# Two weight slabs of a layer's input projection computed inside the DeltaNet scans as native float32 products

## What is computed

```python
def even_mixer(...):
    def prepare(h):
        p = h @ w_in                                   # the input projection, (768 x 1024) @ (1024 x 6656 + 64)
        u = centred_depthwise_conv_silu(p[..., :EV_CONV], conv_w, conv_b)
        z = p[..., EV_CONV:EV_CONV + EV_GATE]          # 2048 gate columns
        small = p[..., EV_CONV + EV_GATE:]             # 64 decay and step inputs
        q, k, v, xs, bm, cm = jnp.split(u, EV_CONV_SPLITS, axis=-1)
        ...
    # DeltaNet scans, both directions, 8 heads;  SSD scans, both directions, 16 heads
    def merge(o_dn, y_ssd, x_ssd, z):
        z_dn, z_ssd = jnp.split(z, [DN_VW], axis=-1)
        o_dn = rms_norm(o_dn, dn_norm) * jax.nn.silu(z_dn)
        y = (y_ssd + ssd_d * x_ssd) * jax.nn.silu(z_ssd)
        ...
# DeltaNet, per chunk:  t = (I + A)^-1 by substitution;  u = t @ (v beta);  w = t @ (k beta exp(g))
```

## Time and profile before

| | us |
|---|---|
| median of 3 runs (lowest, highest) | 2743.19 (2742.74, 2743.46) |
| profiled execution: first to last instruction (span) | 2736.6 |
| median less span: start and end of the execution, which the trace doesn't cover | 6.6 |
| TensorE busy, share of the span | 2536.9, 93% |
| VectorE busy, share of the span | 1610.3, 59% |
| GpSimd busy, share of the span | 955.6, 35% |
| stage in0, about | 60 to 508 |
| DeltaNet g = 0, g = 1, about | 508 to 660, 660 to 803 |

### The profile page before, as it was taken

The page is one execution under the profiler, slowest core; times in us unless marked ns, Lnnn a source line. Parts: engine busy times, 40 slices in busy tenths (PEclk is TensorE's granted clock), DMA queues, the critical chain, the costliest instruction groups (busy, mean ns, idle before and its releaser), DMA issues.

```text
span 2736.6 us, 41739 instructions
## 1 busy us (share of the span) xinstructions
PE 2536.9 (93%) x15718; PEld 2257.2 (82%) x15718; DVE 1610.3 (59%) x2541; ACT 1141.0 (42%) x2081; POOL 955.6 (35%) x515
## 2 busy tenths in 40 slices
PE   7999999868588899899999999999889999899999
PEld 5999999767575588899999987989678877888887
DVE  4988886465867841877777768632666663411111
ACT  4444432435457531433233335433666664322221
POOL 2322223444536522265455533232200012344443
PEclk9999999979799999999999999999999999999999
DMA  7344455203011031123333432333674312132222
GB/s 280 112 139 132 136 168 212 82 25 127 25 45 49 28 135 62 53 94 129 126 132 131 140 107 95 133 104 112 229 244 130 128 34 71 64 106 93 92 99 86
DMA packets 126079, 307.19 MB, mean 112 GB/s; under 512 B 12640, under 2 KB 40800, under 8 KB 124512
## 3 DMA queue, kind: packets, MB, share of 16 engines
q1 hardware_dynamic: 103888, 258.36, 27.9%
q10 hardware_dynamic: 22032, 46.67, 4.9%
HBM read 249.10 MB, written 55.84 MB: 111 GB/s over the span
## 4 chain that ended last, share of the span: by engine, by line
PE 64%; DVE 15%; issue 12%; ACT 6%; POOL 2%; ACTq 1%; DMA 1%; DVEq 0%; SPq 0%; POOLq 0%
PE ps L563 12%; PE ps L564 12%; PE ps L565 12%; DVE ybuf L2785 4%; PE ps L1500 3%; PE ps L1502 3%; PE ps L1501 3%; PE ps L1401 2%; PE ps L1377 2%; PE ps L1387 2%; ACT prb L2160 1%; POOL Wl L544 1%; DVE ps L2858 1%; DVE Vall L2862 1%; DVE ps L2697 1%
## 5 line engine op out<-in xcount | busy, mean ns | idle before, releaser
L544 POOL TENSOR_TENSOR Wl<-raws,Wh 128x2048 fp32r<-128x2048 f32 (+3 forms) x129 | 504.4, 3911 | 1374.3 <-ACT Wh L538 1366.1
L563 PE MATMUL ps<-Hh,Wh 128*128 128x384 f32 (+2 forms) x1152 | 401.8, 349 | 20.9 <-ACT ubuf L1695 12.5
L565 PE MATMUL ps<-Hh,Wl 128*128 128x384 f32 (+2 forms) x1152 | 392.6, 341 | 0.0
L564 PE MATMUL ps<-Hl,Wh 128*128 128x384 f32 (+2 forms) x1152 | 392.6, 341 | 0.0
L538 ACT ACTIVATE Wh<-raws 128x2048 fp32r<-128x2048 f32 (+3 forms) x131 | 209.5, 1600 | 190.7 <-PE ps L565 140.7
L3116 DVE SCALAR_TENSOR_TENSOR xT<-ps,mod,xT 128x384 f32<-128x384 f32 (+3 forms) x174 | 84.5, 534 | 276.2 <-PE ps L565 276.2
L563 PEld LDWEIGHTS ps<-Hh,Wh 128*128 128x128 f32 x1152 | 217.9, 189 | 34.6 <-ACT ubuf L1695 15.0
L564 PEld LDWEIGHTS ps<-Hl,Wh 128*128 128x128 f32 x1152 | 217.9, 189 | 7.0 <-issue 2.6
L565 PEld LDWEIGHTS ps<-Hh,Wl 128*128 128x128 f32 x1152 | 217.8, 189 | 4.8
L2785 DVE SCALAR_TENSOR_TENSOR ybuf<-ubuf,vec,ybuf 128x770 f32<-128x770 f32 x144 | 184.4, 1280 | 43.0 <-ACT ybuf L1701 28.1
L563 PE MATMUL ps<-H1h,Wh 128*128 128x512 f32 (+1 forms) x368 | 142.1, 386 | 3.1 <-DVE H1l L2667 2.0
(11 more groups left out here) (471 smaller groups left out, 6611.5 us busy)
## 6 DMA issues: line engine op xcount, KB each, us to landing
raws<-in_slabs SPq DMA_DIRECT2D x218, 512.0 KB, 4.6
adl<-in_ada ACTq DMA_DIRECT2D x48, 512.0 KB, 3.7
ada<-in_ada SPq DMA_DIRECT2D x32, 512.0 KB, 4.4
raws<-in_slabs SPq DMA_DIRECT2D x54, 256.0 KB, 3.0
chunks<-obuf ACTq DMA_DIRECT2D x52, 256.0 KB, 3.4
ada<-in_ada SPq DMA_DIRECT2D x8, 1024.0 KB, 5.0
chunks<-obuf ACTq DMA_DIRECT2D x52, 128.0 KB, 3.6
chunks<-uh SPq DMA_DIRECT2D x17, 384.0 KB, 2.3
```

The source lines that it names most:

```text
L544: nc.gpsimd.tensor_tensor(Wl[n % 2][:, 0:w], raw[n % 2][:, 0:w], Wh[n % 2][:, 0:w].bitcast(f32), ALU.subtract).then_inc(sig("slab_lo"), 1)
L563: nc.tensor.matmul(o, lhs(c)[0], rhs(c, t0, t1)[0], start=(s == 0), stop=False)
L564: nc.tensor.matmul(o, lhs(c)[0], rhs(c, t0, t1)[1], start=False, stop=False)
L565: last = nc.tensor.matmul(o, lhs(c)[1], rhs(c, t0, t1)[0], start=False, stop=(s == k - 1))
```

## The change

`IN0_SLABS = 24`: stage in0 ends after slab 23. Slabs 24 and 25 are still loaded, but are neither rounded nor split. Each DeltaNet half computes one of them, between the sums of squares and the substitution's result: two chunks, four halves of 384 tokens, each as 8 plain float32 matmuls of the raw slab with the float32 `h` (32 matmuls per half g). So that there is a float32 `h`, GpSimd adds `Hh + Hl` into `xT`, one block after each of `lo_slab` 3 to 10. ScalarE applies silu to the four halves into `gz`, and SP stores them. The loads of `sx`, `sB`, `sC` move behind the second half's products, since they overwrite `xT` and `raws`. The turns 17 to 31 are spread over slabs 19 to 23, three each; `dk`, `dq` are loaded in front of slab 23. A table load is added on ScalarE before the recurrence.

```diff
@@ pe_in0
-            with pe.Fori(1, 12) as i:
+            with pe.Fori(1, (IN0_SLABS - 1) // 2) as i:
...
-            chunk(0, 25, 1)
+            chunk(0, IN0_SLABS - 1, 1)
+        def late_gates(g):
+            per = 26 - IN0_SLABS
+            return [((2 * IN0_SLABS + per * g + c) // 2, (2 * IN0_SLABS + per * g + c) % 2, x, (6, 7, 4, 6)[2 * c + x])
+                    for c in range(per) for x in range(2)]
+        def pe_late_gates(pe, g):
+            for e, (n, cc, x, b) in enumerate(late_gates(g)):
+                if e == 0:
+                    pe.wait_ge(sig(f"slab_in{n % 2}"), 32 * (n // 2 + 1))
+                    pe.wait_ge(sig("dn_kv"), 12 * g + 12)
...
+                for k in range(KD):
+                    ins = nc.tensor.matmul(ps[:, b, 0:HALF], w[:, k, cc * P:(cc + 1) * P], xT[:, k, x * HALF:(x + 1) * HALF],
+                                           start=(k == 0), stop=(k == KD - 1))
+                ins.then_inc(sig("gz_done"), 1)
@@ pe_deltanet
             ins.then_inc(sig("dn_ss"), 1)
+            pe_late_gates(pe, g)
             pe.wait_ge(sig("dn_qs"), g + 1)
             pe.wait_ge(sig("dn_w"), past("dn_w") + 3 * g + 2)
+        def act_late_gates(act, g):
...
+                nc.scalar.activation(gz[cc][:, x * HALF:(x + 1) * HALF], ps[:, b, 0:HALF], ACT.Silu).then_inc(sig("gz_out"), 1)
@@ act_deltanet
+            act_late_gates(act, g)
             act.wait_ge(sig("dn_w"), past("dn_w") + 3 * g + 3)
...
+            nc.scalar.preload_act_table_set("natural_log_exp_and_others")
@@ gpsimd_program
-            with pool.Fori(1, 12) as i:
+            for k in range(KD):
+                lo_slab(pool, 3 + k, 0)
+                nc.gpsimd.tensor_tensor(xT[:, k, :], Hh[:, k, :].bitcast(f32), Hl[:, k, :].bitcast(f32), ALU.add)
+            with pool.Fori(5, (IN0_SLABS - 1) // 2) as i:
@@ sync_program
-                for u in (n - 2,) if n < 19 else range(2 * n - 21, 2 * n - 19 + (n == 25)):
+                turns = 15 * max(n - 19, 0) // (IN0_SLABS - 19), 15 * (n - 18) // (IN0_SLABS - 19)
+                for u in (n - 2,) if n < 19 else range(17 + turns[0], min(17 + turns[1], 32)):
                     load_ada_turn(sp, u)
-                if n == 24:
+                if n == IN0_SLABS - 2:
```

72 lines of the change are left out of this document (50 added, 22 removed).

## The result

The changed kernel takes 2749.3 us (median of 8 runs, 2746.0 to 2754.6) against 2741.9 us of the kernel before on the same chip (8 runs, 2736.3 to 2743.5). The ratio is 1.0031, with a 95% interval of 1.0021 to 1.0040, so 6 to 11 us more. Forecast were 2736.7 us with a range up to 2746.0. The profiled execution has a span of 2748.0 us, 11.4 more than the 2736.6 before.

The account below looks back on a forecast made before the run. A VectorE-ScalarE loop bounds in0's convolution part, TensorE its gate part, latencies DeltaNet. Slabs -33.3, additions +12.0, DeltaNet +13.8, in0's end +1.0 sum to -6.5 us: 2736.7 us against 2743.2, range 2729 to 2746.

Parts of the forecast that it names:

- Two slabs, -33.3: In0's gate part, bound by TensorE: slabs 24 and 25 leave it, 4 chunks x 8.32 = 33.3 us off.
- Additions, +12.0: In0's convolution part: each of eight GpSimd additions costs VectorE 1.50 us, 12.0 us in all.
- The rival with the whole 1.84 us each, 14.7: Convolution part: VectorE loses each addition's full duration, 14.7 us in all, total 2739.4 us; chance 0.14.
- DeltaNet, +13.8: Both DeltaNet halves: 32 float32 products each delay X5, 14.8 - 1.4 + 0.4 = 13.8 us (bounds 9 and 18).
- The end of in0, +1.0: In0's last turn and slab 23 may come slightly late: 1.0 us for both (bounds 0 and 5).
- On SP, the later loads of `sx`, `sB`, `sC` ... nothing: Second DeltaNet half: these loads fall some 70 us before the SSD stage wants them and cost nothing.
- the end of in0 starves: Rival: turn 31 or slab 23 late by 5 us, total 2740.7; chance 0.26 together with upper prices.
- The slow clock in the float32 runs: Rival: both DeltaNet runs stay at 1.2 GHz, 41.4 us each, total 2774.7; chance 0.09 including unseen waits.
- no idle TensorE before L846's counterpart and before slab 23: Sign in in0's gate part: slabs at 16.64 us each, with TensorE never idle at these two places.
- if something outside these stages moves by more than 1 us: Sign that the prediction is wrong: a move of over 1 us outside in0 and DeltaNet.

Follow-up runs that it names:

- e3: The changed kernel with the loads of sx, sB, sC moved behind zbuf's load on SP: 2743.8 us, ratio 1.0012.
- e7: The changed kernel with dk, dq loaded behind the last turns' loads and sx, sB, sC behind zbuf's load: 2737.7 us, ratio 0.9985.
- e8: As e7, but without the additions, the modulated input being made in place in xT: 2724.2 us, ratio 0.9934.
- e9: As e7, but with the eight additions behind the subtractions of slabs 19 to 23, in the gate part: 2727.9 us, ratio 0.9955.
- e11: The kernel before, unchanged, for a second trace and further runs: 2742.8 us, ratio 1.0006.
- e5: The kernel before with nothing but the eight GpSimd additions, behind subtractions 3 to 10: 2754.4 us, ratio 1.0047.

## Why the prediction was wrong

The sum was -6.5 us, and the medians say +7.4 and +8.6. Term by term:

- **Two slabs, -33.3.** Right. From VectorE's first turn of the gate part to DeltaNet it is 123.5 us in both traces of before and 90.2 in the kernel with the input in place (476.16 - 385.94), 33.3 less.
- **Additions, +12.0.** Right in mechanism, a little low in size: 12.65 to 14.0 by the pairs of traces above, I take 13.3. The line between 0.98 us for 512 columns and 4.11 for 2048 gave 1.50 us each, and it was 1.6 to 1.7. The rival with the whole 1.84 us each, 14.7, lies about as far off on the other side.
- **DeltaNet, +13.8.** Right. `X5` came later by 8.4 and 6.6 us behind the sums of squares (forecast 7.6 and 7.2), and took 1.2 and 0.3 us less itself (forecast 1.4 in all). With the loads out of the way (e3, e7, e8, e9) the halves take 90.2 and 93.1 us in the mean, before 84.7 and 84.2 (the mean of before, e11 and e5): +14.4.
- **The end of in0, +1.0: this is the step that failed.** It was 9.0, in both traces of the changed kernel: 99.24 us from the first turn of the gate part to DeltaNet, against 90.2. Of this 7.2 us are idle TensorE and the rest the low clock behind it. The text had the mechanism, "its load stands behind `dk` and `dq`, and `dq` took 16.0 us to land", and then made "0 to 4 us late by my count" and took 1.0. The count isn't written out, but it seems to have given the slab a start over TensorE that it doesn't have: before, the slab in this place had 19 us to spare, and by SP's timeline it lost them to the three turns' blocks that now go out ahead of it, a spread which the text had only counted as a gain for the turns. A slab that landed in 7.9 us was ready at 470, and TensorE wanted it at 470.35, so each microsecond of its 7.5 us of delay counted. The bound of 5 was too small for the same reason, and the clock behind the idle time had no term at all.
- **"On SP, the later loads of `sx`, `sB`, `sC` ... nothing": the second miss.** The prediction asked only whether they would be in time for the SSD stage. They are, but they ran beside the couplings and corners of the second half and cost 2.2 to 2.5 us there. That data transfers can hold up TensorE where it waits for none of them was in no term.
- **3 us in layer 1's attention**, which no term had and no experiment explains (above). They may not belong to the change at all, since the kernel before with nothing but the additions has them too.

Sum: -33.3 + 13.3 + 14.4 + 9.0 + 2.5 + 3 = +8.9, against medians of +7.4 and +8.6. The terms overlap a little with scatter: single stretches of one kernel differ by 1 to 2.5 us, so the fit to within 1 us is partly luck. Of the 15 us between forecast and result, 8 are the end of in0, 3 the attention stage, 2.5 the loads, and 1.9 are sizes.

Of the rivals, "the end of in0 starves" named the right place and gave it 5 us. The slow clock in the float32 runs didn't come. "What would show it" had asked for "no idle TensorE before L846's counterpart and before slab 23", and it is that row which fell. It also called the prediction wrong "if something outside these stages moves by more than 1 us", and that came too.

## What to carry to other kernels

A large transfer directly ahead of a load that the bound engine is about to want costs each microsecond by which it delays that load; here 3 MB made a slab of 1 MB 7.5 us later, and TensorE with it. So for each load of such a stage, work out when it lands and when it is wanted; if it has no start, nothing large may stand ahead of it. Whatever else the queue waits for ahead of the load, here the turns' blocks, takes from its start. When a stall goes, look at what was behind the transfer that caused it: moved by one place it made the next consumer late, moved by two it cost nothing. Work for "idle" GpSimd is paid by VectorE, so put it where VectorE isn't in the loop, or write what is needed in the first place instead of adding it together again: that was worth 13 us.

## What the runs showed of the hardware

- GpSimd and VectorE took turns, operation by operation. An addition of 768 columns took 1.84 us with no VectorE operation in the way and 2.55 to 2.83 us beside one. VectorE's next step took 2.87 us in place of 1.23, and its taps in the same situation 6.17 for four in place of 4.51.
- A float32 product of 128x128 by 128x384 took 0.645 us at the full clock (eight from one copy to the next in 5.16 us), which is the line between 0.22 us for 128 columns and 0.86 for 512.
- In the first trace of the changed kernel the clock rose 5.2 and 3.1 us after the two runs of products began. From the sums of squares to `X5` the traces of the kernels with 32 products show two values only, 29.4 and 31.1 us, in either half. In the attention stage stretches of the same code differ by steps of 1.5 us.
- With the six loads under way (DMA share 1.01) TensorE stood still for 1.2 to 1.5 us with nothing to wait for by the timeline, in all five traces, and in none of the four with the loads moved away. A stall of 1.9 to 2.3 us a little earlier didn't go with them. Both ended 2.2 to 2.6 us after a 16 KB transfer of kind "instruction" began, and the loads made the second of these transfers 2.4 us later. That TensorE waited for instructions is what this suggests; no run tested it.
